# Token rows kept once in fp32 for gathering and final sums, instead of as three bf16 parts

## What is computed

```
x = x + merge @ w_out                                    # 288 x 2048, fp32
h = rms_norm(x, g_ffn)
logits = h @ [w_rg | w_re] + bias                        # 4 groups, 16 experts
top-1 group of 4, then top-2 of its 4 experts; gate weights from two softmaxes
for e in range(16):                                      # D_EXPERT = 512
    a = silu(h @ w_e_gate[e]) * (h @ w_e_up[e])
    y = y + gate[:, e:e+1] * (a @ w_e_down[e])
out = rms_norm(x + y, g_final)
```

## Time and profile before

| | |
|---|---|
| median of 3 runs | 1350.24 us (1347.64 to 1367.45) |
| profiled execution | 1358.27 us, span 1356.6 us |
| mean granted TensorE clock | 0.927 |
| busy: PE / DVE / ACT | 1246.6 / 466.3 / 382.2 us |
| DMA over the span | 340.48 MB, 251 GB/s |
| expert loop (L1028, first to last) | 820.6 to 1291 us |

### The profile page before, as it was taken

How to read it: one execution, slowest core, us unless ns; L and a number is a source line. 1 busy time by engine, 2 the same in 40 slices (tenths; PEclk the granted TensorE clock), 3 DMA queues, 4 the chain that set the end, 5 groups by cost and what they waited for, 6 DMA issues and landing times.

```text
span 1356.6 us, 22796 instructions
## 1 busy us (share of the span) xinstructions
PE 1246.6 (92%) x9452; PEld 984.0 (73%) x9452; DVE 466.3 (34%) x708; ACT 382.2 (28%) x484; POOL 63.0 (5%) x107
## 2 busy tenths in 40 slices
PE   5889999979999999999999969999999999999952
PEld 2789999978888999999999945555555555555520
DVE  2724345643444544544534551011000101001027
ACT  3433333234556554454422450000000000000002
POOL 3100010001112000000000000000000000000010
PEclk9899999998999999999999988888888888889975
DMA  9483544451233345354575256999999999999955
GB/s 268 147 320 127 204 156 170 157 194 39 87 124 124 107 142 173 136 186 162 190 275 186 94 216 247 372 430 427 425 426 427 425 427 428 427 428 429 428 159 151
DMA packets 136015, 340.48 MB, mean 251 GB/s; under 512 B 5024, under 2 KB 107552, under 8 KB 113840
## 3 DMA queue, kind: packets, MB, share of 16 engines
q1 hardware_dynamic: 131648, 319.31, 60.8%
q0 software_dynamic: 3936, 17.23, 4.1%
q10 hardware_dynamic: 400, 3.51, 0.7%
HBM read 319.51 MB, written 20.71 MB: 251 GB/s over the span
## 4 chain that ended last, share of the span: by engine, by line
PE 81%; ACT 5%; DVE 5%; DMA 4%; issue 3%; POOL 0%; ACTq 0%; DVEq 0%; POOLq 0%; SPq 0%
PE bank L1028 16%; PE bank L813 14%; PE bank L815 14%; PE bank L814 14%; PE bank L1049 11%; PE bank L1008 6%; PE bank L1036 2%; ACT wh L585 2%; DMA ring<-in_w_in 2%; DMA yb<-y_rows,rows 1%; DVE wl L1133 1%; PE bank L791 1%; DMA con<-in_const 1%; ACT L653 1%; PE bank L1016 1%
## 5 line engine op out<-in xcount | busy, mean ns | idle before, releaser
L813 PE MATMUL bank<-xh,wh 128*128 128x288 f32 x1088 | 330.8, 304 | 10.7 <-DVE xl L1141 5.8
L814 PE MATMUL bank<-xl,wh 128*128 128x288 f32 x1088 | 323.4, 297 | 0.0
L815 PE MATMUL bank<-xh,wl 128*128 128x288 f32 x1088 | 322.5, 296 | 0.0
L1133 DVE TENSOR_TENSOR wl<-ring,wh 128x2048 fp32r<-128x2048 f32 x100 | 229.2, 2293 | 212.6 <-ACT wh L585 212.5
L585 ACT ACTIVATE wh<-ring 128x2048 fp32r<-128x2048 f32 x100 | 190.9, 1909 | 149.8 <-PE bank L815 138.3
L1028 PE MATMUL bank<-home,hg 128*64 128x512 f32 x1024 | 224.7, 596 | 1.5 <-DVE hg L1403 1.5
L813 PEld LDWEIGHTS bank<-xh,wh 128*128 128x128 f32 x1088 | 206.1, 189 | 15.8 <-issue 8.6
L815 PEld LDWEIGHTS bank<-xh,wl 128*128 128x128 f32 x1088 | 207.2, 190 | 0.0
L814 PEld LDWEIGHTS bank<-xl,wh 128*128 128x128 f32 x1088 | 207.0, 190 | 0.3
L1028 PEld LDWEIGHTS bank<-home,hg 128*64 128x64 f32 x1024 | 90.1, 138 | 132.3 <-issue 132.3
L1049 PE MATMUL bank<-home,aT 128*64 128x512 f32 x512 | 147.6, 737 | 0.5 <-ACT aT L758 0.5
(11 more groups left out here) (284 smaller groups left out, 1085.3 us busy)
## 6 DMA issues: line engine op xcount, KB each, us to landing
ring<-in_w_in SPq DMA_DIRECT2D x34, 2048.0 KB, 8.1
home<-in_w_e_gate SPq DMA_DIRECT2D x64, 1024.0 KB, 12.3
home<-in_w_e_up SPq DMA_DIRECT2D x64, 1024.0 KB, 14.2
home<-in_w_e_down SPq DMA_DIRECT2D x32, 2048.0 KB, 9.9
ring<-in_w_out SPq DMA_DIRECT2D x8, 2048.0 KB, 7.6
ring<-in_w_sb_o SPq DMA_DIRECT2D x8, 1024.0 KB, 5.0
ring<-in_w_swa_o SPq DMA_DIRECT2D x8, 1024.0 KB, 7.2
y_rows<-y_sb SPq DMA_DIRECT2D x32, 256.0 KB, 9.6
```

The costliest lines, as they stand in the source:

```text
L813: mm_(dst, wh[:, j % 2, k, :], hi[:, k, :], start=(k == k0), stop=False)
L814: mm_(dst, wh[:, j % 2, k, :], lo[:, k, :], start=False, stop=False)
L815: mm = mm_(dst, wl[:, j % 2, k, :], hi[:, k, :], start=False, stop=(k == k1 - 1))
L1133: v.tensor_tensor(wl[:, j % 2], raw(j), wh[:, j % 2].bitcast(F32), ALU.subtract)\
```

## The change

The rows are kept once, as one fp32 tile `x2` of 96 x 3 x 2048. DVE copies each PSUM bank into it (`rows_of`), ACT squares from SBUF; nothing is split. `pick` becomes fp32, and the gather, the slot scales and the final sums use the fp32 rows. The multiplication by the identity at the end is gone; L1510 reads the rows themselves. The logits are computed for seven tiles after the second product of the last step, seven after the third, one when tile 14 is ready, and the last one behind `token_major(3)`; ACT copies them to `lgT` between its squares. PE waits for the two converted constants `su_b` and `ones_b` ahead of the ranks. Small tiles of the routing move to other addresses.

```diff
-    x2 = [at(f"x2_{j}", 64 + 12 * j, [P, 3, D], BF16) for j in range(3)]
-    x2r = [at(f"x2r{t}", 132 + 2 * t, [P, 512]) for t in range(3)]
+    x2 = at("x2", 64, [P, 3, D])
-    pick = at("pick", 46, [P, 3, SLOTS], BF16)
+    pick = at("pick", 46, [P, 3, SLOTS])
-    ident_b = at("ident_b", 203.25, [P, P], BF16)
-    rparts = at("rparts", 205.8125, [P, 3, 4], BF16)
...
@@ ScalarE
             for q in range(4):
                 for t in range(3):
-                    act.wait_ge(S["x2_ps"], 3 * q + t + 1)
-                    a_.activation(quarter(0, t, q), by_tile(x2_bank(q, t)[0:TR]), ACT.Copy)
+                    act.wait_ge(S["x2_sb"], 3 * q + t + 1)
                     if q or t:
-                        act.wait_ge(S["x2_a"], 3 * q + t)
-                    a_.activation(squares2[0:TR], x2_bank(q, t)[0:TR], ACT.Square, accum_out=sums2[0:TR, t, q:q + 1])\
-                        .then_inc(S["x2_a"], 1)
-                for t in range(3):
-                    act.wait_ge(S["x2_r"], 3 * q + t + 1)
-                    a_.activation(x2[1][0:TR, t, q * 512:(q + 1) * 512], x2r[t][0:TR], ACT.Copy).then_inc(S["x2_b"], 1)
+                        act.wait_ge(S["x2_sq"], 3 * q + t)
+                    a_.activation(squares2[0:TR], quarter(t, q), ACT.Square, accum_out=sums2[0:TR, t, q:q + 1])\
+                        .then_inc(S["x2_sq"], 1)
+                    if q == 3 and t == 0:
+                        act.wait_ge(S["lg_ps"], 1)
+                        a_.activation(lgT[:], ps[7][0:NL, 0:NT], ACT.Copy).then_inc(S["lgT_done"], 1)
@@ TensorE
                     if 3 * q + t >= 4:
-                        pe.wait_ge(S["x2_r"], 3 * q + t - 3)
+                        pe.wait_ge(S["x2_sb"], 3 * q + t - 3)
...
             for j in range(4):
                 pe.wait_ge(S["ev_d"], EV_OUT_D + 12 + j)
                 products(IT_END - 1, j, mh, ml)
-                if j:
-                    token_major(j - 1)
-                if j == 1:
+                if j < 3:
+                    token_major(j)
+                if j == 0:
                     pe.wait_ge(S["wr_scaled"], 1)
-                if j > 1:
-                    logits(6 * j - 12, 6 * j - 6)
+                if 0 < j < 3:
+                    logits(7 * j - 7, 7 * j)
+            pe.wait_ge(S["ev_d"], EV_OUT_D + KT)
+            logits(14, 15)
             pe.wait_ge(S["ev_d"], EV_OUT_D + KT + 1)
-            logits(12, KT)
             token_major(3)
+            logits(15, KT)
             pe.wait_ge(S["lgT_done"], 1)
...
             pe.wait_ge(S["masks"], 1)
+            pe.wait_ge(S["sums_b"], 2)
...
                 for k in range(k0, k1):
                     for t in range(3):
-                        for j in range(3):
-                            mm_(ps[k // 8][:, (k % 8) * SLOTS:(k % 8 + 1) * SLOTS],
-                                x2[j][0:TR, t, k * P:(k + 1) * P], pick[0:TR, t, :],
-                                start=(t == 0 and j == 0), stop=(t == 2 and j == 2))
+                        mm_(ps[k // 8][:, (k % 8) * SLOTS:(k % 8 + 1) * SLOTS], x2[0:TR, t, k * P:(k + 1) * P],
+                            pick[0:TR, t, :], start=(t == 0), stop=(t == 2))
...
                 for t in range(3):
-                    for j in range(3):
-                        mm = mm_(ps[3][0:SLOTS, 0:1], pick[0:TR, t, :], rparts[0:TR, j, t:t + 1],
-                                 start=(t == 0 and j == 0), stop=(t == 2 and j == 2))
+                    mm = mm_(ps[3][0:SLOTS, 0:1], pick[0:TR, t, :], stat[0:TR, 8 + t:9 + t],
+                             start=(t == 0), stop=(t == 2))
...
-                for q in range(4):
-                    for j in range(3):
-                        mm = mm_(ps[4 * t % 8 + q][0:TR, :], ident_b[0:TR, 0:TR], x2[j][0:TR, t, q * 512:(q + 1) * 512],
-                                 start=(j == 0), stop=(j == 2))
-                mm.then_inc(S["x2_back"], 1)
@@ VectorE
-            def parts(q):
+            def rows_of(q):
 
                 for t in range(3):
-                    dve.wait_ge(S["x2_a"], 3 * q + t + 1)
...
-                for t in range(3):
-                    dve.wait_ge(S["x2_b"], 3 * q + t + 1)
-                    v.tensor_tensor(x2[2][0:TR, t, q * 512:(q + 1) * 512], x2r[t][0:TR],
-                                    x2[1][0:TR, t, q * 512:(q + 1) * 512], ALU.subtract).then_inc(S["x2_d"], 1)
+                    dve.wait_ge(S["x2_ps"], 3 * q + t + 1)
+                    v.tensor_copy(quarter(t, q).rearrange("t (k p) -> t k p", k=KPC), by_tile(x2_bank(q, t)[0:TR]))\
+                        .then_inc(S["x2_sb"], 1)
...
-            dve.wait_ge(S["lg_ps"], 1)
-            v.tensor_copy(lgT[:], ps[7][0:NL, 0:NT]).then_inc(S["lgT_done"], 1)
-            parts(3)
...
+            rows_of(3)
+            dve.wait_ge(S["x2_sq"], 12)
...
                 dve.wait_ge(S[f"y_in{t}"], 32)
-                dve.wait_ge(S["x2_back"], t + 1)
...
-                                           in1=ps[4 * t % 8 + q][0:n, :].rearrange("t (k p) -> t p k", k=KPC),
+                                           in1=quarter(t, q).rearrange("t (k p) -> t p k", k=KPC),
```

## The result

The changed kernel takes 1549.03 us (median of 4 runs, 1545.45 to 1550.85) where the kernel before, on the same chip, takes 1358.29 (1347.64 to 1367.45): a ratio of 1.1397, 95% interval 1.1324 to 1.147. Over all comparisons the runs of the kernel before fall into two groups, 1346.8 to 1358.3 us and 1363.6 to 1369.6, so its median moves with how many fall in each. Ratios are formed from the runs, not from the medians beside them. The profiled execution took 1548.26 us with a span of 1546.5, and its mean granted clock is 0.872.

What follows compares the result with a forecast made beforehand. TensorE and the expert-weight transfers were taken to bound the expert loop side by side. From 1358.3 us, +164 (loop), +13.5 (first gather) and -2 (routing) gave 1534, or 1526 for the median; range 1465 to 1585.

Steps and rivals of the forecast that it cites:

- The period: Loop over 16 experts: one expert's TensorE work takes 41.4 us; fifteen make 621 us, 164 more than 457.25.
- The price: fp32 gather: each weight load takes 112 ns at full clock and 213 at half, 96 instructions an expert.
- The clock: Expert loop: the granted clock falls to half 5.0 us into the gather and stays down; chance 0.60.
- the sum's own rival: Expert loop: the clock falls only behind L1036, periods of 38.7 us, 1485 us in all; chance 0.20.
- The sum: Whole kernel: loop +164, first gather +13.5, routing -2, giving 1534 us profiled and 1526 for the median.
- First gather: Gather ahead of the first expert: at half clock throughout, 20.4 us instead of 6.99, 13.5 more.
- Routing: Stretch behind the last turn of the tokens: fewer operations bring the root near 801.4, 2.0 us gained.
- The end: Final sums: removing 36 matmuls gains nothing; reading SBUF instead of PSUM costs at most some tenths in four operations.
- The clock stays up: Rival for the loop: full clock all the time, periods of 33.85 us, 1405 us in all; chance 0.13.
- holds until L1036: Rival for the loop: clock full until L1036 has run, periods of 38.7 us, 1485 in all; chance 0.20.
- Not slower: Rival for the gather: loads below 79 ns at full clock, transfers set the period, 1350 us; chance 0.04.
- Worse: Rival for the gather: loads at 251 ns throughout, periods of 49.6 us, 1652 us in all; chance 0.03.

Runs made afterwards that it cites:

- e7: Changed kernel with pick standing twice side by side for feature tiles 0 to 11, 128 moving columns instead of 64 behind the same weight loads: 1477.89 us.
- b2: Kernel before the change with each bf16 gather instruction done twice in a row, a longer gather that is as dense: 1414.93 us.
- e1: Changed kernel with TensorE's wait for the scaled logit weights moved back behind the second product of the last projection step: 1545.66 us.
- e3: Changed kernel with the next expert's first 36 gather matmuls put tile by tile behind the gate and up products of tiles 3 to 14: 1574.52 us.

## Why the prediction came out

**The period, 41.4 predicted, 41.74 measured.** Term by term against the period shown: 72 gather instructions 10.8 against 10.43 (10.1 to 11.6 in the loop, 10.84 on average); L1032 2.0 against 2.06; 24 more 5.1 against 5.31; slot scales 0.6 against 0.62; L1045 9.2 against 9.14. The price came from rows of another stage, 112 and 213 ns a load; the gather's loads start exactly so far apart. That a load of 128 contiguous fp32 columns has a price that doesn't depend on the columns that follow was carried over from 32 columns to 64, and e7 shows it for 128.

**The clock.** Predicted to fall 5.0 us into the gather, it falls after 4.3 to 5.9, on average 5.1. That the value fits is in part luck: it was taken between two rows that had no gather in them. That the waiting for loads is the reason, not the length, was only argued then. b2 rules out the length. e7 shows that the pace of the loads isn't the whole reason either: at the same 112 ns, with twice the columns behind each load, the clock held through the 72. The step that no row showed, that the clock falls inside the gather and not behind L1036, is worth 41 us by the sum's own rival (1485).

**L1032.** The sum left open whether it doubles at half clock; it doesn't (2.06 at 0.50, 2.01 at 1.00).

**First gather.** 20.4 predicted, 20.71 measured; its surroundings +14.1 against 13.5.

**Routing, the step that failed.** Predicted -2.0, measured +3.1; the root came at 808.2 instead of 801.4. What the sum did count was right, as e1 shows with -1.8. What the sum missed stands in the diff: the wait for `wr_scaled` moved from `j == 1` to `j == 0`. The prediction followed the logits and the transposes past the products, but not this wait, behind which three of four products are queued on PE. L1294, its releaser, stands behind the split of the next weights on VectorE.

**The end, mis-sized.** Predicted nothing, measured +2.25. That L1510 had waited only 0.47 us for the row DMA was read as "nothing to gain"; it also meant that there was next to no cover if the sums grew. They grew by 1.4 us a third. The words "at most some tenths in four operations" treated a read from SBUF as one from PSUM and passed over its step.

**The sum.** 164 + 13.5 - 2 = 175.5 predicted between the profiled executions, 190.0 measured. The 14.5 between them are 5 from the period (15 times 0.33), 0.6 from the first gather, 5.1 from routing, 2.25 from the end and 1.6 from code that wasn't changed. All point the same way. Of the 5, 3 are the 24 instructions behind L1032 (5.31 against 5.1) and 1.9 the first expert's products, begun at half clock (15.60 against 13.73); the other terms of the period nearly cancel. The forecast of 1526 stood against a median of 1350.24; the kernel before has 1358.29 beside the changed one, so 8 of the 23 us between 1526 and 1549 are its own.

**Rivals.** "The clock stays up" (1405) and "holds until L1036" (1485) fall by the windows above. "Not slower" asked for loads under 79 ns apart; they stand 112 apart at full clock. "Worse", 251 ns throughout, would need the stepped loads of L1032.

## What to carry to other kernels

Count weight loads, not instructions: three bf16 products with loads at 30 ns are cheaper than one fp32 matmul, which has two loads at 112 ns, and once the clock has fallen in such a stretch each load takes 213. When a diff moves a wait, look up what its releaser stands behind on its own engine and what is queued behind the waiter. When a multiplication that also moved data to PSUM is taken away, look at how the next reader steps through it.

## What the runs showed of the hardware

Two things were not expected. A gather's loads did not start under the 512-column products before them: a change to the gather and back cost 0.29 us (e3). And with 128 instead of 64 moving columns behind each fp32 load, the loads kept their 112 ns and the clock held through all 72 (e7): wasted columns made the kernel 71 us faster. How the chip decides when the clock falls isn't settled by these runs.
